# Making the low parts of the down products' weights with an adding transfer in a two-block transformer kernel

## The chip, the core and the metric

The kernel runs on one core of one Trainium2 chip. The metric is the device time of one execution in microseconds (us). Three timed runs of the kernel before gave a median of 1833.34 us (1831.85 to 1833.65).

The engines named below are TensorE (PE in the profile; its weight loads are PEld), VectorE (DVE), ScalarE (ACT), GpSimd (POOL) and SyncE (SP, which here only issues transfers).

## The reference

One sequence of 512 tokens with 1024 features passes through two blocks of two layers each, in float32. The first block has a stick-breaking attention layer and a latent attention layer. In the second block each layer has a mixer (first a sparse one, then a differential one) and then this MLP, which is the part that the change touches:

```python
def sq_relu_mlp(h, w_up, w_down):
    u = jnp.einsum('btd,df->btf', h, w_up)
    return jnp.einsum('btf,fd->btd', jnp.square(jax.nn.relu(u)), w_down)

h = h + sq_relu_mlp(rms_norm_2(h, mlp_norm_g[layer]), mlp_w_up[layer], mlp_w_down[layer])
```

`w_up` is 1024 x 4096 and `w_down` is 4096 x 1024, so each layer has 32 blocks of 128 x 1024 numbers of down weights; there are two layers.

## The kernel before

**Three products for one.** TensorE multiplies in a reduced format (`fp32r`, called FR in the code). To keep float32 accuracy, each matrix is split into a high part (the value rounded to fp32r) and a low part (the value minus its high part), and each product is made of three: high x high, low x high and high x low (the helper `three`). The activations' parts of the MLP are HIDH and HIDL.

**The stream of weight blocks.** Weights come as blocks of 128 x 1024 float32 numbers (512 KB) in one fixed stream, numbered b. For each block

- SP loads the raw numbers into one of two buffers (`load`, WRAW, NR = 2),
- ACT makes the high part in one of three buffers (`split_high`, WH, NS = 3) once TensorE has used block b - 3,
- DVE, or POOL for some blocks outside the MLPs, makes the low part (`split_low`, WL, also three buffers),
- TensorE waits for both parts and uses the block.

A raw buffer may be loaded again when the low part of the block in it is made (`at("low", b - NR)` in `load`).

**The MLP.** A layer's hidden features come in four quarters c = 0 to 3. Quarter 0 goes the plain way: eight up blocks m = 0 to 7 with 24 matmuls of 512 columns each. Its results are scaled by DVE (line 2476), squared and split by ACT (lines 2520 and 2522), and their low parts are made by POOL (line 2552, HIDL<-TMP,HIDH). For m > 3 POOL then also mixes four planes of the input (`plane_mix`, lines 2341, 2344 and 2347), which quarters 1 to 3 need: their up products are made by a fast scheme with fewer matmuls, in eight steps of 42 matmuls of 256 columns (`fast_pe`). Each quarter ends with eight down blocks m = 0 to 7 of 24 matmuls of 512 columns, called down m below. TensorE's order for them is: down 0 without its last two k, down 1 without its last two k, the rest of down 0, the rest of down 1, then down 2 to 7 whole. `low` of the first three down blocks of quarter 0 is made in the last three rounds of `mlp_vector`'s first loop, those of the other quarters in rounds 6 to 8 of its fast loop; the others follow as TensorE frees their buffers.

**Order.** Each engine runs its own list of instructions in the order in which it is written, and waits only at semaphores. The order is written out by hand in `mlp_tensor`, `mlp_vector`, `mlp_scalar` and `mlp_gpsimd`; nothing is planned by costs. POOL has no work in an MLP other than its first loop.

Of the kernel before, what the change touches and what calls it, by code (L numbers as in the profile page):

```python
# [8 lines left out]
F32 = mybir.dt.float32  # L9
FR = mybir.dt.float32r  # L10
BF16 = mybir.dt.bfloat16
ALU = mybir.AluOpType
# [12 lines left out]
NR, NS = 2, 3  # L25
# [111 lines left out]
def program(nc, A, out):  # L137
    ctx = ExitStack()
    with ctx:
# [114 lines left out]
        on_pool |= {block[("o_v", b), half] for b in range(1, 4) for half in range(2)}  # L254

        def load(e, w, b):
            if b >= NR:
                w.wait_ge(*at("low", b - NR))
            name, i, width, _ = stream[b]
            e.dma_start(WRAW[b % NR][:, 0:width], A[name][i]).then_inc(*dma(f"s_w{b % NR}"))  # L260

        def split_high(e, w, b):
            if b >= len(stream):
                return
            n = stream[b][2]
            w.wait_ge(*dma(f"s_w{b % NR}", b // NR + 1))
            if b >= NS:
                w.wait_ge(*at("used", b - NS))
            e.activation(WH[b % NS][:, 0:n], WRAW[b % NR][:, 0:n], ACT.Copy).then_inc(*inc("s_high", ("high", b)))  # L269

        def split_low(e, w, b, pool):
            if b >= len(stream) or (b in on_pool) != pool:
                return
            n = stream[b][2]
            if b >= NS:
                w.wait_ge(*at("used", b - NS))
            w.wait_ge(*at("high", b))
            e.tensor_tensor(WL[b % NS][:, 0:n], WRAW[b % NR][:, 0:n], WH[b % NS][:, 0:n].bitcast(F32),  # L278
                            ALU.subtract).then_inc(*inc("s_low_pool" if pool else "s_low", ("low", b)))
# [26 lines left out]
        def tile_t(e, w, name, m, hi, lo, need, kt=KT):  # L306

            per = BW // (128 * kt)
            b = block[name, m // per]
            wh, wl = (x[b % NS][:, 0:BW].rearrange("p (k n) -> p k n", k=kt) for x in (WH, WL))  # L310
            bank, was = banks.take((name, m), ("evac", name, m))
            w.wait_ge(*at("high", b))
            w.wait_ge(*at("low", b))
            for key in was:
                w.wait_ge(*at(*key))
            c = slice(128 * (m % per), 128 * (m % per) + 128)
            made = three(e, w, bank, [(wh[:, k, c], wl[:, k, c], hi(k), lo(k), need(k)) for k in range(kt)])
            ends = [("used", b)] * (m % per == per - 1)
            made.then_inc(*inc("s_tile", ("tile", name, m), *ends))

        def tile_n(e, w, name, hi, lo, need, cols=256):
# [7 lines left out]
            for half in range(2):  # L329
                b = block[name, half]  # L330
                wh, wl = (x[b % NS][:, 0:BW].rearrange("p (k n) -> p k n", k=4) for x in (WH, WL))
                w.wait_ge(*at("high", b))
                w.wait_ge(*at("low", b))
                for i in range(NT):
                    made = three(e, w, bk[i][:, 0:cols],
                                 [(hi(k)[:, tok[i]], lo(k)[:, tok[i]], wh[:, k % 4, :], wl[:, k % 4, :], need(k))
                                  for k in range(4 * half, 4 * half + 4)], half == 0, half == 1)
                    ends = [("tile", name, i)] * (half == 1) + [("used", b)] * (i == NT - 1)
                    if ends:
                        made.then_inc(*inc("s_tile", *ends))  # L340
# [211 lines left out]
        def out_sets(e, w, name, layer, m, ks, bank=None):  # L552
# [3 lines left out]
            w.wait_ge(*at("high", b))  # L556
            w.wait_ge(*at("low", b))
            if ks[0] == 0:
# [48 lines left out]
        def l0_tensor(e, w):  # L607
# [12 lines left out]
            def linear(name, m):  # L620
# [4 lines left out]
                w.wait_ge(*at("high", b))  # L625
                w.wait_ge(*at("low", b))
                for key in was:
# [394 lines left out]
        def l1_tensor(e, w):  # L1022
# [91 lines left out]
            w.wait_ge(*at("high", b))  # L1114
            w.wait_ge(*at("low", b))
            for i in range(NT):
# [414 lines left out]
        def l2_tensor(e, w):  # L1531
            need = need_h("mix0")

            def linear(t, bank):
# [4 lines left out]
                w.wait_ge(*at("high", b))  # L1539
                w.wait_ge(*at("low", b))  # L1540
                for key in was:
# [12 lines left out]
            def natural(half):  # L1554
# [8 lines left out]
                w.wait_ge(*at("high", b))  # L1563
                w.wait_ge(*at("low", b))
                for i in range(NT):
# [14 lines left out]
            def compress(which, q):  # L1580
# [6 lines left out]
                w.wait_ge(*at("high", b))  # L1587
                w.wait_ge(*at("low", b))
                w.wait_ge(*at("window hi", which))
# [16 lines left out]
            def second(which):  # L1606
# [5 lines left out]
                w.wait_ge(*at("high", b))  # L1612
                w.wait_ge(*at("low", b))
                made = three(e, w, bank[:, 0:62], [(wh[:, k, :], wl[:, k, :], EHH[:, k, :], EHL[:, k, :],
# [818 lines left out]
        def mlp_tensor(e, w, L):  # L2433
# [6 lines left out]
            def down(c, m, ks):  # L2440
                b = block[("dn", L, c), m]
                wh, wl = (x[b % NS][:, 0:BW].rearrange("p (k n) -> p k n", k=KT) for x in (WH, WL))
                w.wait_ge(*at("high", b))
                w.wait_ge(*at("low", b))
                if ks[0] == 0:
# [103 lines left out]
        def mlp_gpsimd(e, w, L):  # L2549
            for m in range(8):  # L2550
# [3 lines left out]
                if m > 3:  # L2554
                    plane_mix(e, w, L, m - 4)


# [61 lines left out]
        def l3_tensor(e, w):  # L2619
# [17 lines left out]
            def linear():  # L2637

                for name, m in o_slots:
                    b = block[name, m]  # L2640
                    w.wait_ge(*at("high", b))
                    w.wait_ge(*at("low", b))
                    if name in ("o_q", "o_k"):
# [474 lines left out]
        def end_tensor(e, w):  # L3118
# [4 lines left out]
            def part(x, ks):  # L3123
# [4 lines left out]
                w.wait_ge(*at("high", b))  # L3128
                w.wait_ge(*at("low", b))
                for k in ks:  # L3130
# [367 lines left out]
```

## Time and profile before

| what | value |
|---|---|
| median of three runs | 1833.34 us |
| the profiled execution | 1832.36 us |
| its span (first to last instruction) | 1830.3 us |
| TensorE busy | 1786.5 us (98%) |
| VectorE busy | 1153.7 us (63%) |
| ScalarE busy | 866.5 us (47%) |
| GpSimd busy | 447.4 us (24%) |
| high parts of weights on ScalarE (line 269) | 214 of 1044 ns |
| low parts of weights on VectorE (line 278) | 201 of 1286 ns |

Matmuls are pipelined, so a busy TensorE is not one at its peak: the distance from one matmul's start to the next's is what a matmul costs. What a wait costs is read from TensorE's rows, since TensorE is the engine that hardly rests. A row of a timeline has the start and the length in us, the engine, the line of the kernel, the operation, what it writes and reads, its shape and count, and in brackets the idle time ahead of it and what ended that. "DMA to landing" is from the issue of a transfer to the moment when its semaphore is full.

### The profile page before, as it was taken

Reading aid. Unit: us, or ns where it says so; the run is one execution under the profiler, and the core shown is the slowest. Engines: PE = TensorE matmul, PEld = TensorE weight load, DVE = VectorE, ACT = ScalarE, POOL = GpSimd, SP = SyncE. Lnnn points to the kernel's source line nnn. Section 1 sums busy time; section 2 is a strip of 40 time slices with the busy share of each in tenths; the row PEclk is TensorE's granted clock in tenths of the full one; section 3 lists DMA queues with packets and bytes.
Section 4 is the critical chain, followed back from the end, with each engine's and each line's share of the span. In section 5 each row is a group of like instructions: output and inputs, shape, how many; then the busy total and the mean of one; then the engine's idle time right before and its main releaser. Section 6 shows DMA issues by size and latency. Waiting matters only on the chain.

```text
span 1830.3 us, 26599 instructions
## 1 busy us (share of the span) xinstructions
PE 1786.5 (98%) x10528; PEld 1466.9 (80%) x10532; DVE 1153.7 (63%) x1869; ACT 866.5 (47%) x1409; POOL 447.4 (24%) x451
## 2 busy tenths in 40 slices
PE   7999999999999999999999999999999999999997
PEld 6987777766678757677889898988888788989896
DVE  5355555575545688854577585765677656858574
ACT  5236665355435465564345352533444534435253
POOL 0035551011311235551140000005678214000000
PEclk9999999999999999999999999999999999999999
DMA  5221111231012421111232322222222123232322
GB/s 183 95 67 50 55 50 58 81 97 53 24 47 89 136 67 36 35 36 58 81 115 93 115 93 104 84 99 83 87 89 76 50 81 127 82 115 93 106 91 81
DMA packets 44522, 149.22 MB, mean 82 GB/s; under 512 B 6000, under 2 KB 6384, under 8 KB 44400
## 3 DMA queue, kind: packets, MB, share of 16 engines
q1 hardware_dynamic: 44400, 147.53, 24.0%
q8 instruction: 84, 1.38, 0.3%
q14 instruction: 38, 0.31, 0.0%
HBM read 139.64 MB, written 2.10 MB: 77 GB/s over the span
## 4 chain that ended last, share of the span: by engine, by line
PE 86%; DVE 6%; ACT 3%; POOL 2%; issue 2%; DMA 0%; POOLq 0%; SPq 0%; DVEq 0%; ACTq 0%
PE BANK L301 18%; PE BANK L303 18%; PE BANK L302 18%; PE BANK L2382 4%; PE BANK L2383 4%; PE BANK L2380 4%; PE BANK L933 3%; PE BANK L667 2%; PE BANK L1717 1%; PE BANK L1698 1%; PE BANK L1674 1%; PE BANK L990 1%; PE BANK L2713 1%; PE BANK L652 1%; PE BANK L2688 1%
## 5 line engine op out<-in xcount | busy, mean ns | idle before, releaser
L269 ACT ACTIVATE WH<-WRAW 128x1024 fp32r<-128x1024 f32 (+1 forms) x214 | 222.9, 1044 | 341.4 <-PE BANK L303 312.5
L278 DVE TENSOR_TENSOR WL<-WRAW,WH 128x1024 fp32r<-128x1024 f32 (+1 forms) x201 | 258.3, 1286 | 131.2 <-ACT WH L269 130.9
L301 PE MATMUL BANK<-HH,WH 128*128 128x512 f32 x664 | 273.1, 411 | 12.0 <-DVE WL L278 9.8
L303 PE MATMUL BANK<-HL,WH 128*128 128x512 f32 x664 | 260.2, 392 | 0.0
L302 PE MATMUL BANK<-HH,WL 128*128 128x512 f32 x664 | 259.9, 391 | 0.0
L301 PE MATMUL BANK<-HIDH,WH 128*128 128x512 f32 (+1 forms) x520 | 201.4, 387 | 1.6 <-issue 1.5
L302 PE MATMUL BANK<-HIDH,WL 128*128 128x512 f32 (+1 forms) x520 | 200.9, 386 | 0.0
L303 PE MATMUL BANK<-HIDL,WH 128*128 128x512 f32 (+1 forms) x520 | 200.8, 386 | 0.0
L2383 PE MATMUL BANK<-HP,G 128*128 128x256 f32 x672 | 190.5, 283 | 0.0
L2382 PE MATMUL BANK<-HP,G 128*128 128x256 f32 x672 | 190.5, 283 | 0.0
L2380 PE MATMUL BANK<-HP,G 128*128 128x256 f32 x672 | 190.4, 283 | 0.0
L495 DVE TENSOR_TENSOR X<-X,BANK 128x512 f32<-128x512 f32 x95 | 65.2, 686 | 167.7 <-PE BANK L303 167.7
L301 PEld LDWEIGHTS BANK<-HH,WH 128*128 128x128 f32 x664 | 125.4, 189 | 46.2 <-issue 21.5
L303 PEld LDWEIGHTS BANK<-HL,WH 128*128 128x128 f32 x664 | 125.1, 188 | 27.0
L302 PEld LDWEIGHTS BANK<-HH,WL 128*128 128x128 f32 x664 | 125.5, 189 | 25.4 <-issue 2.9
L2380 PEld LDWEIGHTS BANK<-HP,G 128*128 128x128 f32 x672 | 129.2, 192 | 0.2
L2382 PEld LDWEIGHTS BANK<-HP,G 128*128 128x128 f32 x672 | 129.2, 192 | 0.2
L2383 PEld LDWEIGHTS BANK<-HP,G 128*128 128x128 f32 x672 | 129.2, 192 | 0.0
L301 PEld LDWEIGHTS BANK<-HIDH,WH 128*128 128x128 f32 x520 | 97.8, 188 | 22.6 <-issue 3.2
L303 PEld LDWEIGHTS BANK<-HIDL,WH 128*128 128x128 f32 x520 | 97.8, 188 | 19.8
L302 PEld LDWEIGHTS BANK<-HIDH,WL 128*128 128x128 f32 x520 | 97.8, 188 | 19.2
L2322 ACT ACTIVATE G<-RAW 128x1792 fp32r<-128x1792 f32 x32 | 54.5, 1703 | 88.2 <-DVE RAW L2314 69.0
(446 smaller groups left out, 3755.3 us busy)
## 6 DMA issues: line engine op xcount, KB each, us to landing
WRAW<-in_w SPq DMA_DIRECT2D x77, 512.0 KB, 3.5
WRAW<-in_wd SPq DMA_DIRECT2D x64, 512.0 KB, 3.5
RAW<-in_wf SPq DMA_DIRECT2D x32, 512.0 KB, 3.6
WRAW<-in_wu SPq DMA_DIRECT2D x16, 512.0 KB, 3.4
TMP<-in_wf SPq DMA_DIRECT2D x16, 512.0 KB, 3.5
WRAW<-in_w0o SPq DMA_DIRECT2D x8, 512.0 KB, 3.5
WRAW<-in_w1o SPq DMA_DIRECT2D x8, 512.0 KB, 3.4
WRAW<-in_wc SPq DMA_DIRECT2D x8, 512.0 KB, 3.4
```

The lines of the kernel that those rows point to most:

```text
L269: e.activation(WH[b % NS][:, 0:n], WRAW[b % NR][:, 0:n], ACT.Copy).then_inc(*inc("s_high", ("high", b)))
L278: e.tensor_tensor(WL[b % NS][:, 0:n], WRAW[b % NR][:, 0:n], WH[b % NS][:, 0:n].bitcast(F32), ALU.subtract).then_inc(*inc("s_low_pool" if p ...
L301: e.matmul(dst, ah, bh, start=first and i == 0, stop=False)
L302: e.matmul(dst, al, bh, start=False, stop=False)
L303: made = e.matmul(dst, ah, bl, start=False, stop=last and i == len(sets) - 1)
L495: e.tensor_tensor(X[:, m, :], X[:, m, :], banks[name, m], ALU.add).then_inc(*inc("s_evac", ("evac", name, m)))
L667: made = e.matmul(l0_bank(h, bk)[:, c0 + 128 * (jj - j):c0 + size[j]], ntri if jj == j else nones, nlf[:, h % 2, col[jj]:col[jj] + size[jj ...
L933: made = e.matmul(bank[:, c], a, b, start=(i == 0), stop=(i == len(sets) - 1), skip_group_check=True)
L2322: e.activation(flat(G[s % 3][:, 0:7, :]), raw_part(s, 1, 7), ACT.Copy).then_inc(*inc("s_fast_high", ("fast high", L, s)))
L2380: e.matmul(dst, wh[:, a, cols], hi, start=half == 0 and j not in started, stop=False, skip_group_check=True)
L2382: e.matmul(dst, wl[:, a, cols], hi, start=False, stop=False, skip_group_check=True)
L2383: made = e.matmul(dst, wh[:, a, cols], lo, start=False, stop=half == 1 and i == 1, skip_group_check=True)
```

## The change

For the 64 down blocks, DVE no longer makes the low part. ACT, right after it has written the high part, writes its negative into the low buffer (a second activation with scale -1, `s_minus`). Then POOL issues a transfer (`add_raw`) that reads the raw block from memory a second time and adds it onto the low buffer, so that this holds raw minus high. TensorE waits for the semaphore of that transfer in place of `low` (`low_made`). SP may reload a raw buffer as soon as the high part of its block is made (`raw_read`). No other block is changed.

```diff
+        added = [b for b, (_, _, _, key) in enumerate(stream) if key[0][0] == "dn"]
+        def low_made(b):
+            if b in added:
+                return dma(f"s_low_added{b % NS}", 1 + sum(a % NS == b % NS for a in added if a < b))
+            return at("low", b)
+        def raw_read(b):
+            return at("high", b) if b in added else at("low", b)
         def load(e, w, b):
             if b >= NR:
-                w.wait_ge(*at("low", b - NR))
+                w.wait_ge(*raw_read(b - NR))
...
         def split_high(e, w, b):
             e.activation(WH[b % NS][:, 0:n], WRAW[b % NR][:, 0:n], ACT.Copy).then_inc(*inc("s_high", ("high", b)))
+            if b in added:
+                w.wait_ge(*at("high", b))
+                e.activation(WL[b % NS][:, 0:n], WH[b % NS][:, 0:n].bitcast(F32), ACT.Copy, scale=-1.0).then_inc(
+                    *inc("s_minus", ("minus high", b)))
+        def add_raw(e, w, b):
+            name, i, n, _ = stream[b]
+            w.wait_ge(*at("minus high", b))
+            e.dma_start(WL[b % NS][:, 0:n], A[name][i], accum_op=ALU.add).then_inc(*dma(f"s_low_added{b % NS}"))
         def split_low(e, w, b, pool):
-            if b >= len(stream) or (b in on_pool) != pool:
+            if b >= len(stream) or b in added or (b in on_pool) != pool:
                 return
...
         def mlp_gpsimd(e, w, L):
                 if m > 3:
                     plane_mix(e, w, L, m - 4)
+                if m > 4:
+                    add_raw(e, w, block[("dn", L, 0), m - 5])
+            for c in range(4):
+                for m in range(8):
+                    if c or m > 2:
+                        add_raw(e, w, block[("dn", L, c), m])
```

Every wait of TensorE for `at("low", b)` became one for `low_made(b)`.

POOL, the end of a layer's first loop (rounds m = 4 to 7), before:

```order
181 L2552 TENSOR_TENSOR HIDL<-TMP,HIDH 128x512 x5
182 L2341 TENSOR_TENSOR STAGE<-STAGE 128x512
183 L2344 TENSOR_TENSOR STAGE<-STAGE 128x256
184 L2347 TENSOR_TENSOR STAGE<-STAGE 128x256
185 L2552 TENSOR_TENSOR HIDL<-TMP,HIDH 128x512
186 L2341 TENSOR_TENSOR STAGE<-STAGE 128x512
187 L2344 TENSOR_TENSOR STAGE<-STAGE 128x256
188 L2347 TENSOR_TENSOR STAGE<-STAGE 128x256
189 L2552 TENSOR_TENSOR HIDL<-TMP,HIDH 128x512
190 L2341 TENSOR_TENSOR STAGE<-STAGE 128x512
191 L2344 TENSOR_TENSOR STAGE<-STAGE 128x256
192 L2347 TENSOR_TENSOR STAGE<-STAGE 128x256
```

The same place on POOL with the change:

```order
185 L2572 TENSOR_TENSOR HIDL<-TMP,HIDH 128x512
186 L2361 TENSOR_TENSOR STAGE<-STAGE 128x512
187 L2364 TENSOR_TENSOR STAGE<-STAGE 128x256
188 L2367 TENSOR_TENSOR STAGE<-STAGE 128x256
189 L289 DMA WL<-in_wd 128x1024
190 L2572 TENSOR_TENSOR HIDL<-TMP,HIDH 128x512
191 L2361 TENSOR_TENSOR STAGE<-STAGE 128x512
192 L2364 TENSOR_TENSOR STAGE<-STAGE 128x256
193 L2367 TENSOR_TENSOR STAGE<-STAGE 128x256
194 L289 DMA WL<-in_wd 128x1024
195 L2572 TENSOR_TENSOR HIDL<-TMP,HIDH 128x512
199 L289 DMA WL<-in_wd 128x1024 x30
```

The first adding transfer stands behind the second plane mix, the second behind the third, and the other thirty of the layer behind the fourth.

ACT, from the last fast steps to the first down blocks of a later quarter, with the change:

```order
594 L2441 ACTIVATE Q<-Q 128x1024
595 L2443 ACTIVATE Q<-Q 128x1024
596 L2445 ACTIVATE HIDH<-Q 128x1024
597 L280 ACTIVATE WH<-WRAW 128x1024
598 L283 ACTIVATE WL<-WH 128x1024
599 L2413 ACTIVATE Q<-BANK 128x256
600 L280 ACTIVATE WH<-WRAW 128x1024
601 L283 ACTIVATE WL<-WH 128x1024
602 L2441 ACTIVATE Q<-Q 128x1024
603 L2443 ACTIVATE Q<-Q 128x1024
604 L2445 ACTIVATE HIDH<-Q 128x1024
605 L280 ACTIVATE WH<-WRAW 128x1024
```

Each high part (line 280, before line 269) is followed at once by its negative (line 283), which is new; the rest keeps its order.

## Rows read from the trace of the kernel before

**Rows 1.** The page: span and busy time of the engines (us, share, count).

```profile
span 1830.3 us, 26599 instructions
PE 1786.5 (98%) x10528; PEld 1466.9 (80%) x10532; DVE 1153.7 (63%) x1869; ACT 866.5 (47%) x1409; POOL 447.4 (24%) x451
```

**Rows 2.** Busy time by stretch: columns PE, PEld, DVE, ACT, POOL, clock, DMA share, GB/s.

```profile
880.00:923.30 43.30, 43.24 (x189) 35.15 (x188) 25.81 (x31) 16.34 (x23) 13.33 (x10) 1.00 0.21 73
923.30:968.20 44.90, 44.14 (x194) 36.28 (x195) 32.57 (x35) 20.83 (x18) 13.40 (x11) 1.00 0.35 128
1008.40:1052.00 43.60, 43.60 (x195) 36.12 (x194) 22.68 (x31) 13.16 (x11) 0.00 (x0) 1.00 0.33 119
```

**Rows 3.** TensorE's timeline where down 0 and down 1 of quarter 0 begin.

```profile
921.04 0.39 PE L301 MATMUL BANK<-HH,WH 128*128 128x512 f32 x1
...
922.85 0.39 PE L303 MATMUL BANK<-HL,WH 128*128 128x512 f32 x1
923.31 0.47 PE L301 MATMUL BANK<-HIDH,WH 128*128 128x512 f32 x1
...
928.43 0.47 PE L301 MATMUL BANK<-HIDH,WH 128*128 128x512 f32 x1 [0.75 <-issue]
```

**Rows 4.** POOL's timeline at the same place (rounds 5 and 6).

```profile
922.08 2.27 POOL L2341 TENSOR_TENSOR STAGE<-STAGE 128x512 f32<-128x512 f32 x1
...
925.25 0.74 POOL L2347 TENSOR_TENSOR STAGE<-STAGE 128x256 f32<-128x256 f32 x1
925.95 1.30 POOL L2552 TENSOR_TENSOR HIDL<-TMP,HIDH 128x512 fp32r<-128x512 f32 x1
```

**Rows 5.** ACT's timeline there: the high part of down 0's block.

```profile
920.65 1.04 ACT L269 ACTIVATE WH<-WRAW 128x1024 fp32r<-128x1024 f32 x1
```

**Rows 6.** DVE's timeline there: the low part of down 1's block.

```profile
926.12 2.21 DVE L278 TENSOR_TENSOR WL<-WRAW,WH 128x1024 fp32r<-128x1024 f32 x1 [2.31 <-ACT WH L269]
```

**Rows 7.** Transfers in 968 to 1052 us: packets, MB, share; KB each, us to landing.

```profile
q1 hardware_dynamic: 2326, 8.45, 28.9%
WRAW<-in_wd SPq DMA_DIRECT2D x8, 512.0 KB, 3.5
```

**Rows 8.** TensorE's timeline where down 0 of quarter 1 begins.

```profile
1008.31 0.40 PE L301 MATMUL BANK<-HIDH,WH 128*128 128x512 f32 x1
```

**Rows 9.** ACT's timeline in quarter 1, from the last fast step on.

```profile
1004.88 1.04 ACT L269 ACTIVATE WH<-WRAW 128x1024 fp32r<-128x1024 f32 x1
...
1009.84 1.06 ACT L2421 ACTIVATE Q<-Q 128x1024 f32<-128x1024 f32 x1 [2.46 <-DVE Q L2415]
1010.94 1.06 ACT L2423 ACTIVATE Q<-Q 128x1024 f32<-128x1024 f32 x1
...
1018.11 1.06 ACT L269 ACTIVATE WH<-WRAW 128x1024 fp32r<-128x1024 f32 x1 [5.02 <-PE BANK L303]
```

**Rows 10.** TensorE's first matmuls, after 9.78 us of idle time.

```profile
9.78 0.76 PE L301 MATMUL BANK<-HH,WH 128*128 128x512 f32 x1 [9.78 <-DVE WL L278]
10.35 0.63 PE L302 MATMUL BANK<-HH,WL 128*128 128x512 f32 x1
...
13.70 0.40 PE L301 MATMUL BANK<-HH,WH 128*128 128x512 f32 x1
```

**Rows 11.** Busy time by stretch after TensorE's last matmul (columns as rows 2).

```profile
1822.00:1822.50 0.50, 0.00 (x0) 0.00 (x0) 0.29 (x2) 0.47 (x2) 0.00 (x0) 1.00 0.00 0
1823.00:1823.50 0.50, 0.00 (x0) 0.00 (x0) 0.50 (x3) 0.00 (x0) 0.50 (x2) 0.50 0.00 0
```

**Rows 12.** POOL's timeline in the second layer: the end of its second plane mix.

```profile
1524.04 0.74 POOL L2347 TENSOR_TENSOR STAGE<-STAGE 128x256 f32<-128x256 f32 x1
```

**Rows 13.** TensorE's timeline in the second layer: the start of its down 0.

```profile
1522.09 0.47 PE L301 MATMUL BANK<-HIDH,WH 128*128 128x512 f32 x1
```

**Rows 14.** The issue of a plain transfer on SP.

```profile
1043.83 0.33 SPq L2304 DMA_DIRECT2D TMP<-in_wf  x1
```

**Rows 15.** Transfers of the whole execution: the four that load X at its start.

```profile
X<-in_x SPq DMA_DIRECT2D x4, 512.0 KB, 6.9
```

More of the change, by code:

```diff
@@ L312, in tile_t @@
             w.wait_ge(*at("high", b))
-            w.wait_ge(*at("low", b))
+            w.wait_ge(*low_made(b))
             for key in was:
@@ L332, in tile_n @@
                 w.wait_ge(*at("high", b))
-                w.wait_ge(*at("low", b))
+                w.wait_ge(*low_made(b))
                 for i in range(NT):
@@ L556, in out_sets @@
             w.wait_ge(*at("high", b))
-            w.wait_ge(*at("low", b))
+            w.wait_ge(*low_made(b))
             if ks[0] == 0:
@@ L625, in linear @@
                 w.wait_ge(*at("high", b))
-                w.wait_ge(*at("low", b))
+                w.wait_ge(*low_made(b))
                 for key in was:
@@ L1114, in l1_tensor @@
             w.wait_ge(*at("high", b))
-            w.wait_ge(*at("low", b))
+            w.wait_ge(*low_made(b))
             for i in range(NT):
@@ L1539, in linear @@
                 w.wait_ge(*at("high", b))
-                w.wait_ge(*at("low", b))
+                w.wait_ge(*low_made(b))
                 for key in was:
@@ L1563, in natural @@
                 w.wait_ge(*at("high", b))
-                w.wait_ge(*at("low", b))
+                w.wait_ge(*low_made(b))
                 for i in range(NT):
@@ L1587, in compress @@
                 w.wait_ge(*at("high", b))
-                w.wait_ge(*at("low", b))
+                w.wait_ge(*low_made(b))
                 w.wait_ge(*at("window hi", which))
@@ L1612, in second @@
                 w.wait_ge(*at("high", b))
-                w.wait_ge(*at("low", b))
+                w.wait_ge(*low_made(b))
                 made = three(e, w, bank[:, 0:62], [(wh[:, k, :], wl[:, k, :], EHH[:, k, :], EHL[:, k, :],
@@ L2443, in down @@
                 w.wait_ge(*at("high", b))
-                w.wait_ge(*at("low", b))
+                w.wait_ge(*low_made(b))
                 if ks[0] == 0:
@@ L2641, in linear @@
                     w.wait_ge(*at("high", b))
-                    w.wait_ge(*at("low", b))
+                    w.wait_ge(*low_made(b))
                     if name in ("o_q", "o_k"):
@@ L3128, in part @@
                 w.wait_ge(*at("high", b))
-                w.wait_ge(*at("low", b))
+                w.wait_ge(*low_made(b))
                 for k in ks:
```

## The prediction, made before the changed kernel was run

> **What bounds the kernel.** I read the page first. TensorE is busy for 1786.5 of 1830.3 us; DVE, which loses work, for 63% [rows 1]. So time taken off DVE is worth only what TensorE waits for DVE. I then cut the MLP of layer 0 into stretches [rows 2]: up tiles (880 to 923.3), down tiles of quarter 0 (923.3 to 968.2), down tiles of quarter 1 (1008.4 to 1052). TensorE has work in all of 43.3, in 44.14 of 44.9 and in all of 43.6 us. A matmul of 512 columns costs (922.85 - 921.04) / 8 = 0.226 us [rows 3], 24 of them 5.44 us, and eight tiles 43.5. Quarter 1 takes just that, quarter 0 some 1.3 more. TensorE's timeline shows where: about 0.2 us ahead of down 0 at 923.31, and 0.75 ahead of down 1 at 928.43 [rows 3]. The latter is the wait for its low part, which DVE ends at 926.12 + 2.21 = 928.33 [rows 6]. That is all DVE can give back: about 1 us a layer, 2 in all. What counts is whether the new chain for the low part is as early as the old.
>
> **What goes and comes.** DVE loses 64 instructions of some 1.2 to 2.2 us, which the above says is worth at most 2 us, and only if nothing later takes the wait's place. ACT gains 64 of 1.06 us. In the 43.6 us of quarter 1's down tiles ACT is busy for 13.16 [rows 2]; the new ones add 8.5 at most, so its throughput is no issue, only its place in the chain. SP's loads may start a DVE instruction earlier; nothing waits for them. POOL issues 64 transfers. DMA is 33% busy in that stretch [rows 2]: 2326 packets of queue 1 are 8.45 MB, 16 transfers of 512 KB, in 0.289 x 84 us, so one keeps the 16 engines busy for 1.5 us [rows 7]. An adding one reads memory and the buffer: 3.0. With the load, 4.5 per 5.44 us: it fits, with little to spare.
>
> **The unknown, D.** D is the time from POOL's reaching an adding transfer to its full semaphore. The trace has none, nor any transfer issued by POOL. Nearest: a plain one of the same size takes 3.5 us [rows 7]. That is the lower end, as adding needs all that a copy needs and a second read. The four loads of X at the start, which share the engines with others, take 6.9 [rows 15]; that is not an upper bound, since how fast the adder is, and how POOL makes its orders, no row shows. As an outer end I take 8.3, at which (below) the chain would fill the time between three blocks; beyond it the loss grows faster. Between the ends I add: 3.5, plus 1.5 for the second read, plus about 1.0 for sharing with the plain load that the new rule releases at nearly the same moment. D = 6.0. POOL itself is held for q per issue: SP's issue takes 0.33 [rows 14], I take 1.0, at most 2.0.
>
> What memory moves is a matter for a page: in the Trainium skill, "Collectives: The Full Stack" (the bandwidth ceiling) says that the add costs no cycles but two reads on one ring, which halves the rate; "DMA: Bandwidth & Descriptors" (Latency) gives a transfer issued by GpSimd about 2 us plus its bytes over 436 GB/s. An estimate from both pages is 2 + 2 x 1.2 = 4.4 us, and the sum below would end at 1849. No run here shows it yet.
>
> **Quarter 0, twice.** This is where order counts. POOL's new list has the first transfer behind its second plane mix. That mix ends at 925.95, 2.64 us after TensorE stood ready for down 0 at 923.31 [rows 3, 4]. The negative is no obstacle: the high part starts at 920.65 and takes 1.04 [rows 5], two of them end at about 922.9. In before DVE had made this low part by then. So down 0 starts at 925.95 + D = 931.95. POOL goes on with a HIDL of 1.29 and a mix of 925.95 - 922.08 = 3.8 [rows 4], so the second transfer comes q + 5.12 later, at 932.07, and lands at 938.07; the third comes at 938.2.
>
> TensorE has rested for 8.6 us. At the kernel's start, after 9.78 us without work, its first nine matmuls are 0.43 us apart (1.2 GHz) before the distance becomes 0.23 (2.4 GHz): 3.92 us for what takes 2.04 [rows 10]; after its last matmul the granted clock is 1.00 at 1822.0 and 0.50 at 1823.0 [rows 11]. So I charge 1.9 us for slow matmuls. By the Trainium skill, "TensorE: Matmul & The Clock Gate" (Part 1), an idle array falls to half its clock; those rows agree. Without that rule the sum would be at most 3.8 less.
>
> Down 0 without its last two k is 18 matmuls: 4.08 + 1.9, to 937.93. Down 1 waits to 938.07, runs to 942.15. The rests end at 943.5 and 944.9; down 2 runs 944.9 to 950.3. The buffer of down 3 is free at 943.5; as in quarter 1 the high part starts 0.28 later, two activations take 1.10 + 1.06 [rows 9], POOL gets the signal 0.06 later, and it lands at 952.0. Down 3 started at 968.2 - 0.3 - 5 x 5.44 = 940.7 in before; now at 952.0: 11.3 us late. Downs 4 to 7 have 10.88 us from free buffer to use, less 0.28 + 2.16 + 0.06, so they hold up to D = 8.3 and wait for nothing. The second layer repeats it: the mix ends at 1524.78, TensorE is ready at 1522.09 [rows 12, 13]. Twice 11.3 = 22.6.
>
> **Quarters 1 to 3, six times.** Down 0 starts at 1008.31 [rows 8]. Two places are tight. Down 1, due 4.08 us later at 1012.39: its high part starts at 1004.88 [rows 9], its negative is ready at 1007.1, so 5.3 us are there for D. Down 3, due at 1008.31 + 72 x 0.2267 = 1024.63: since TensorE interleaves downs 0 and 1, its buffer is free only at 1017.8; the high part starts at 1018.11, the negative is ready at 1020.3, 4.3 us are there. In before, DVE needed 1.2. At D = 6: 0.7 + 1.7 = 2.4 us, six times: 14.4. These waits are short; I charge no clock.
>
> **The sum.** 22.6 + 14.4 = 37.0. The profiled execution took 1832.36, so 1869.4; the median shown is 1.0 above it: 1870. The same steps for other D: 3.5 gives 14.2 (1847), 5.0 gives 22.8 (1855), 7.0 gives 53.1 (1885), 8.3 gives 73.9 (1906), 10 gives 114 (1946). If q is 2.0, add 2 us.
>
> **Rivals.**
> First, a quick transfer (D under 5): only quarter 0's place behind the mixes costs. For it: the plain one's 3.5, and engines 67% idle. 1847 to 1855. 20%.
> Second, the middle, D from 5 to 7.5: 1855 to 1893, my forecast. 52%.
> Third, the transfer becomes a bound (D over 7.5, or over 5.4 us of the engines' time): then most downs wait, not two per quarter, and each us of D over 8.3 costs about 24 us, (114 - 73.9) / 1.7. For it: nothing in the trace shows the adder's rate. Against: the engines have two thirds of their time. 1893 to 1950 or more. 24%.
> Fourth, not slower: POOL reaches the transfer in time. It would have to land by 923.3, so with the lowest D the second mix would have to end at 919.8, 6.2 us before the 925.95 of the rows and 2.3 us before that mix begins at 922.08 [rows 4]. Then quarter 0 gives its 1 us back, and if D is below 4.3 the rest costs nothing: 1833.3 - 2 = 1831. It decides at the order of POOL's list alone, and that order is against it. 3%.
> That the change doesn't do what it says (a block still split by DVE) is excluded by the lists; the last 1% is for what I have not thought of.
>
> **Chances and range.** What a measurement of this kernel can tell from no change is about 0.2%, 3.7 us. The first three all lie over it: 96% slower, 2% the same, 2% faster. The range reaches from the first's lower edge to 1925, some way into the third; 15% are left out, nearly all above.
>
> **What would show it.** In the profile after: TensorE's first matmul of down 0 in quarter 0 waits 6 to 9 us for the transfer of WL, in both layers, and the next nine or so are 0.43 apart; POOL's issue stands directly behind the second mix. In later quarters down 1 and down 3 wait, the others not. The line of adding transfers gives D's landing time: near 6 if I am right. TensorE's wait for DVE at down 1 is gone. I am wrong if down 0 doesn't wait (order), if waits stand at every down tile (D or the rate too low), or if the plain loads' 3.5 us grow beyond 5, which would move waits to the high parts.

## The result and the profile after

The changed kernel takes 1908.47 us, the median of four runs (1905.14 to 1911.56); the kernel before took 1832.74 us in four runs beside it. The ratio is 1.040, with a 95% interval of 1.038 to 1.042. It is slower by 76 us where 37 were forecast. The profiled execution took 1905.14 us.

The page of the changed kernel: span, busy time of the engines, the queues, TensorE's largest group, the adding transfers (line 289; what ended POOL's idle time before them), and two lines of its list of transfers (count, KB each, median us from issue to landing).

```profile
span 1903.3 us, 26667 instructions
PE 1803.9 (95%) x10532; PEld 1474.6 (77%) x10532; DVE 1074.5 (56%) x1805; ACT 932.2 (49%) x1473; POOL 498.1 (26%) x515
...
q1 hardware_dynamic: 44400, 147.53, 23.8%
q0 software_dynamic: 9216, 33.56, 10.0%
...
L321 PE MATMUL BANK<-HIDH,WH 128*128 128x512 f32 (+1 forms) x520 | 208.5, 401 | 57.7 <-issue 53.7
...
L289 POOL DMA_DIRECT2D WL<-in_wd x64 | 55.9, 874 | 564.9 <-ACT WL L283 564.9
...
WRAW<-in_wd SPq DMA_DIRECT2D x64, 512.0 KB, 4.3
...
WL<-in_wd POOLq DMA_DIRECT2D x64, 512.0 KB, 7.4
```

Against [rows 1], DVE gave 79 us of busy time and ACT took 66, as meant, and neither shows in the time. The span grew by 73.0 us, TensorE's busy time by 17.4. A matmul's busy time is counted longer while the clock is low, so this is a first sign of slow matmuls; the remaining 55.6 us are rest. Queue 0 is the adding transfers: 33.56 MB in 64 pieces, 0.100 x 1903.3 / 64 = 2.97 us of all 16 engines for each. From issue to landing one takes 7.4 us in the median (5.1 to 10.3). The plain loads of the same blocks now take 4.3 instead of 3.5 [rows 7].

The view of waits names 14 large waits in a group that it could put down to nothing (issue), 53.7 us together, the longest 10.3:

```profile
PE BANK L321 <- issue: 53.7, 14, 10.3
```

TensorE's timeline shows what they are. Columns: start, length, engine, line, operation, and in brackets the rest before it and what ended it.

```profile
922.69 0.39 PE L323 MATMUL BANK<-HL,WH 128*128 128x512 f32 x1
933.43 0.77 PE L321 MATMUL BANK<-HIDH,WH 128*128 128x512 f32 x1 [10.35 <-issue]
933.99 0.63 PE L322 MATMUL BANK<-HIDH,WL 128*128 128x512 f32 x1
934.42 0.63 PE L323 MATMUL BANK<-HIDL,WH 128*128 128x512 f32 x1
...
953.66 0.47 PE L321 MATMUL BANK<-HIDH,WH 128*128 128x512 f32 x1 [1.59 <-issue]
965.60 0.47 PE L321 MATMUL BANK<-HIDH,WH 128*128 128x512 f32 x1 [0.73 <-DMA WL<-in_wd]
1029.11 0.47 PE L321 MATMUL BANK<-HIDH,WH 128*128 128x512 f32 x1 [2.49 <-issue]
1046.90 0.69 PE L321 MATMUL BANK<-HIDH,WH 128*128 128x512 f32 x1 [3.67 <-issue]
1139.03 0.66 PE L321 MATMUL BANK<-HIDH,WH 128*128 128x512 f32 x1 [3.84 <-issue]
1567.71 0.77 PE L321 MATMUL BANK<-HIDH,WH 128*128 128x512 f32 x1 [9.12 <-issue]
```

The first row is the last up tile of quarter 0, the second is down 0, 10.5 us late. 953.66 is down 3 and 965.60 down 5 of quarter 0. 1029.11 is down 1 and 1046.90 down 3 of quarter 1; 1139.03 is down 3 of quarter 2. The last row is down 0 of quarter 0 in the second layer. POOL's timeline holds the other side:

```profile
920.67 1.30 POOL L2572 TENSOR_TENSOR HIDL<-TMP,HIDH 128x512 fp32r<-128x512 f32 x1 [1.41 <-ACT HIDH L2542]
921.93 1.29 POOL L2361 TENSOR_TENSOR STAGE<-STAGE 128x512 f32<-128x512 f32 x1
923.30 0.73 POOL L2364 TENSOR_TENSOR STAGE<-STAGE 128x256 f32<-128x256 f32 x1
924.11 0.72 POOL L2367 TENSOR_TENSOR STAGE<-STAGE 128x256 f32<-128x256 f32 x1
924.78 1.02 POOL L289 DMA_DIRECT2D WL<-in_wd  x1
929.88 0.87 POOL L289 DMA_DIRECT2D WL<-in_wd  x1
...
1021.54 0.86 POOL L289 DMA_DIRECT2D WL<-in_wd  x1 [6.63 <-ACT WL L283]
...
1039.03 0.88 POOL L289 DMA_DIRECT2D WL<-in_wd  x1 [14.31 <-ACT WL L283]
```

The first transfer stands directly behind the second mix, as the order of the list has it. It is issued at 924.78 and lands 8.6 us later, when down 0 starts. The one issued at 1021.54 lands 7.5 us later, at 1029.0, and down 1 starts at 1029.11. The one at 1039.03 takes 7.8, to 1046.8, and down 3 starts at 1046.90. Whatever the view calls them, the 17 waits of 0.7 us and more in the two MLPs all end 0.09 to 0.13 us after an adding transfer has landed.

The granted clock, in three stretches (columns as in [rows 2]):

```profile
925.00:926.00 1.00, 0.00 (x0) 0.00 (x0) 0.00 (x0) 1.00 (x2) 1.00 (x2) 1.00 0.38 61
927.00:928.00 1.00, 0.00 (x0) 0.00 (x0) 0.00 (x0) 0.98 (x2) 1.00 (x2) 0.76 0.97 242
1029.00:1031.00 2.00, 1.89 (x6) 1.60 (x7) 0.00 (x0) 0.00 (x0) 0.00 (x0) 0.73 0.92 182
```

TensorE rested from 923.1 and the clock fell from its upper level (2.4 GHz) to the lower (1.2 GHz) within 927 to 928. After the 2.5 us of rest ahead of 1029.11 it fell as well, on the way through 1029 to 1031. From 1029.88 to 1033.26 the matmuls start 0.43 us apart, in place of 0.23.

Adding up the starts of TensorE's matmuls over both MLPs gives the balance. The waits, counted from start to start less the usual distance of 0.23, are 60.4 us (24.3 in the two quarters 0, 36.0 in the six later ones), the slow matmuls cost 14.0 (4.4 and 9.6), and before had 2.2 of both. 60.4 + 14.0 - 2.2 = 72.2, of the 73.0 by which the span grew. Slow matmuls follow both long waits and six of the twelve waits at down 1 and down 3 of the later quarters.

### The profile page after: what moved, and what is told of

It reads as the page before. It is cut to its first block, busy times and chain, and to the rows that moved or that the text cites. A ratio compares the mean times of both kernels' runs of the same rounds, so it can differ in the third digit from the quotient of the medians.

```text
span 1903.3 us, 26667 instructions
## 1 busy us (share of the span) xinstructions
PE 1803.9 (95%) x10532; PEld 1474.6 (77%) x10532; DVE 1074.5 (56%) x1805; ACT 932.2 (49%) x1473; POOL 498.1 (26%) x515
## 3 DMA queue, kind: packets, MB, share of 16 engines
q0 software_dynamic: 9216, 33.56, 10.0%
## 4 chain that ended last, share of the span: by engine, by line
PE 78%; DVE 7%; ACT 6%; issue 5%; POOL 2%; DMA 2%; POOLq 0%; SPq 0%; DVEq 0%; ACTq 0%
PE BANK L321 16%; PE BANK L322 15%; PE BANK L323 15%; PE BANK L2403 4%; PE BANK L2402 4%; PE BANK L2400 4%; PE BANK L953 2%; PE BANK L687 2%; ACT WH L280 2%; DVE WL L298 1%; PE BANK L1737 1%; PE BANK L1718 1%; PE BANK L1694 1%; PE BANK L1010 1%; PE BANK L2739 1%
## 5 line engine op out<-in xcount | busy, mean ns | idle before, releaser
L321 PE MATMUL BANK<-HIDH,WH 128*128 128x512 f32 (+1 forms) x520 | 208.5, 401 | 57.7 <-issue 53.7
L298 DVE TENSOR_TENSOR WL<-WRAW,WH 128x1024 fp32r<-128x1024 f32 (+2 forms) x137 | 173.7, 1269 | 104.9 <-ACT WH L280 104.1
L322 PE MATMUL BANK<-HIDH,WL 128*128 128x512 f32 (+1 forms) x520 | 206.3, 397 | 0.0
L323 PE MATMUL BANK<-HIDL,WH 128*128 128x512 f32 (+1 forms) x520 | 205.4, 395 | 0.0
L289 POOL DMA_DIRECT2D WL<-in_wd x64 | 55.9, 874 | 564.9 <-ACT WL L283 564.9
```

What stands on the lines that cost most here:

```text
L289: e.dma_start(WL[b % NS][:, 0:n], A[name][i], accum_op=ALU.add).then_inc(*dma(f"s_low_added{b % NS}"))
L321: e.matmul(dst, ah, bh, start=first and i == 0, stop=False)
L322: e.matmul(dst, al, bh, start=False, stop=False)
L323: made = e.matmul(dst, ah, bl, start=False, stop=last and i == len(sets) - 1)
```

## The experiments

The kernel before took 1832.6 to 1833.4 us on the chips used. Where no interval stands, a kernel ran once; after's four runs lie within 3.4 us of their median, so I read nothing from less than about 5 us; experiment 3 shows how much of that is the clock.

**1. The first transfer ahead of the mix**

```diff
-                if m > 3:
-                    plane_mix(e, w, L, m - 4)
                 if m > 4:
                     add_raw(e, w, block[("dn", L, 0), m - 5])
+                if m > 3:
+                    plane_mix(e, w, L, m - 4)
```

> The changed kernel with POOL's first three adding transfers ahead of the plane mix of their round, not behind it. If the place in POOL's list decides when down 0 of quarter 0 starts: the first transfer is issued when its negative is ready, at about 922.7 instead of 924.8, and down 0 starts about 2.1 us earlier in each layer; about 4 us less in all, 1901 against 1905. If ACT's chain (or the transfer's own length) decided alone and POOL's order did not matter: the first issue stays within 0.5 us of 924.8 and the time within 1 us of 1905.

1902.48 us, 6 under after's median and 2.7 under its profiled execution. POOL's first issue, and TensorE's start of down 0:

```profile
922.88 1.03 POOL L289 DMA_DIRECT2D WL<-in_wd  x1 [0.99 <-ACT WL L283]
```
```profile
929.02 0.77 PE L321 MATMUL BANK<-HIDH,WH 128*128 128x512 f32 x1 [6.03 <-issue]
```

The issue now waits for the negative (922.88) and no longer for the mix (924.78). Down 0 starts 4.4 us sooner: 1.9 of them are the order, 2.5 are this transfer's length, 6.1 instead of 8.6. That length differs from run to run: it is 7.1, 7.7 and 7.9 in experiments 3, 6 and 7, whose edits don't touch POOL's list or the plain loads. Waits and slow matmuls of the two quarters 0 are 6 us less together. In the six later quarters, which have the same instructions as after, they are 3 us more, nearly all of it slow matmuls, and this is within what differs from run to run. The order costs a few us; it isn't where the 76 went.

**2. A plain copy in place of the addition** (the low part is then the raw weight)

```diff
-            e.dma_start(WL[b % NS][:, 0:n], A[name][i], accum_op=ALU.add)
+            e.dma_start(WL[b % NS][:, 0:n], A[name][i])
```

> The changed kernel with POOL's transfers as plain copies of the raw weights into the low buffer, in the same place, with the same waits, without the adding (the low parts are then not the low parts). If the second read that adding needs, and the engines' time for it, makes the transfer long: one alone lands after about 3.7 to 4.2 us instead of 5.2, the ones in bursts after about 5 instead of 7.5, each takes half the engines' time (1.5 us instead of 3.0), and the kernel takes about 1855 (the sum of the prediction at 5). If POOL's way of issuing is what is long: landing stays at 5 alone and 7 in bursts, and the kernel takes 1895 or more.

1874.58 us: between the two expectations. The page and the view of this line:

```profile
q0 software_dynamic: 9216, 33.56, 5.9%
...
L289 POOL DMA_DIRECT2D WL<-in_wd x64 | 34.5, 539 | 550.7 <-ACT WL L283 550.7
...
DMA to landing us min/median/max: 3.6/4.8/9.0
```

A copy issued by POOL takes 3.7 us alone, almost what SP's take [rows 7], and 0.059 x 1872.6 / 64 = 1.7 us of the engines against 2.97 with the addition. At down 1 and down 3 of quarter 1 it takes 5.8 and 5.6 us, against 7.5 and 7.8. So some 34 of the 76 us are the adding, and some 42 remain with a copy of the same bytes through the same chain.

**3. Source and destination of one type**

```diff
-            e.dma_start(WL[b % NS][:, 0:n], A[name][i], accum_op=ALU.add)
+            e.dma_start(WL[b % NS][:, 0:n], A[name][i].bitcast(FR), accum_op=ALU.add)
```

> The changed kernel with the source of the adding transfer named in the low buffer's own type (fp32r), so that no conversion of type is asked for; the bits added are the same. If the conversion were what makes the transfer long, one alone would land in under 4.5 us and the kernel take 1880 or less. If only reads and writes count: the same landing times within 0.3 us (5.2 alone, 7.4 median) and 1905 within 4.

1909.01 us, and landing in 7.2 us in the median. That the transfer goes from float32 to fp32r costs nothing that these runs can tell.

The run shows one thing more. Its waits are 55.7 us, 4.7 less than in after's profiled execution, but its slow matmuls cost 22 us and not 14.0. So what the clock takes differs by some 8 us between two executions with nearly the same waits. After's own four runs go with it: 1905.14 us at a mean granted clock of 0.988, 1911.56 at 0.984.

**4. One adding transfer at a time**

```diff
             w.wait_ge(*at("minus high", b))
+            if b - 1 in added:
+                w.wait_ge(*low_made(b - 1))
             e.dma_start(WL[b % NS][:, 0:n], A[name][i], accum_op=ALU.add)
```

> The changed kernel, but POOL issues an adding transfer only when the one before it has landed. If bursts on the 16 engines make those of down 1 and down 3 long (7.5 to 7.9 us, while one alone takes 5.2): these two fall to about 6, TensorE waits some 1.5 to 2 us less at each, and with six quarters the kernel takes about 1885. If a transfer's length is its own (issuing, latency), they stay at 7.5 and the kernel takes 1905 or more, since later ones are now issued later.

1943.47 us. That is on the side of the second expectation, but I had expected neither this size nor this place, and its reason, a length of the transfer's own, does not stand either (experiments 9 and 10). POOL's issues for downs 1, 2 and 4 of quarter 1:

```profile
1026.44 0.86 POOL L291 DMA_DIRECT2D WL<-in_wd  x1 [6.62 <-ACT WL L283]
1034.64 0.86 POOL L291 DMA_DIRECT2D WL<-in_wd  x1 [7.33 <-DMA WL<-in_wd]
...
1052.20 0.88 POOL L291 DMA_DIRECT2D WL<-in_wd  x1 [7.25 <-DMA WL<-in_wd]
```

Down 1's still takes 7.6 us, though no other adding transfer is in flight; down 2's, held back until that has landed, takes 5.3. So another adding transfer is not the neighbour that makes down 1's long. Holding each one back makes the later ones late: down 4's could have gone out at 1050.5 and went out at 1052.20, beside three loads of the fast steps' weights; it took 9.3 us. New waits came up at down 4, of 1.4 to 3.2 us in five of the later quarters and of 4.8 and 4.9 in the quarters 0.

**5. DVE makes the tight ones again**: down 1 and down 3 everywhere, and down 0 of quarter 0; 46 blocks are left to the transfer

```diff
-        added = [b for b, (_, _, _, key) in enumerate(stream) if key[0][0] == "dn"]
+        added = [b for b, (_, _, _, key) in enumerate(stream) if key[0][0] == "dn"
+                 and key[1] not in (1, 3) and not (key[0][2] == 0 and key[1] == 0)]
...
         def add_raw(e, w, b):
+            if b not in added:
+                return
```

> The changed kernel, but DVE makes the low parts of down 1 and down 3 in every quarter and of down 0 in quarter 0, as before the change; the other 46 of 64 blocks still go by transfer. If the loss sits in the few places where the chain is longer than TensorE's cover: nearly all of it goes, 1833 within 4. If the transfers' amount (the engines' rate, POOL, ACT's extra instruction) costs: two thirds of the loss stay in proportion to the blocks, 1880 or more.

1863.55 us, a ratio of 1.0175 (1.016 to 1.019). It gives back 45 of the 76 us, not all. In quarter 0, POOL and TensorE show what is late next:

```profile
935.50 1.04 POOL L292 DMA_DIRECT2D WL<-in_wd  x1
```
```profile
941.36 0.76 PE L324 MATMUL BANK<-HIDH,WH 128*128 128x512 f32 x1 [5.56 <-issue]
```

The first transfer is now down 2's. It stands behind POOL's fourth mix in the list, goes out at 935.50, takes 5.8 and down 2 waits for it. Down 5 waits too, 1.2 to 2.5 us, in the quarters 0 to 2 of both layers: in quarter 1 its transfer goes out at 1037.12 beside three loads of the fast steps' weights and takes 10.4 us. I had priced these places by their room in after, in which TensorE itself ran late.

**6. Work in the waits**: 36 matmuls whose result is thrown away ahead of down 0 of quarter 0, and 8 ahead of down 1 and down 3 of the others

```diff
-                w.wait_ge(*low_made(b))
                 if ks[0] == 0:
...
+                    more = {0: 36 if c == 0 else 0, 1: 8 if c else 0, 3: 8 if c else 0}.get(m, 0)
+                    if more:
+                        w.wait_ge(*at("hid hi", L, c, 0))
+                    for _ in range(more):
+                        e.matmul(banks[("dn", L, c), m], wh[:, 0, :], hid_plane(0, 0), start=True, stop=True,
+                                 skip_group_check=True)
+                w.wait_ge(*low_made(b))
```

> The changed kernel with extra matmuls whose results are thrown away, put ahead of TensorE's wait for the low part: 36 at down 0 of quarter 0 and 8 at down 1 and at down 3 of the other quarters (about 8.2 and 1.8 us at full clock, less than the waits of 10 and 2.5 to 3.8 us there). If half of the time lost beside the waits is the slow clock after them: the matmuls behind the waits are 0.23 us apart, not 0.43, and of the 14 us of slow matmuls 10 or more go: 1895 or less. If the slow matmuls are not caused by the rest ahead of them: 1905, or more by what the extra matmuls cost.

1891.42 us: 17 us less than after's median and 13.7 less than its profiled execution, though TensorE does more. TensorE at down 1 of quarter 1:

```profile
1024.73 1.97 PE L2472 MATMUL BANK<-HIDH,WH 128*128 128x512 f32 x8
1027.70 0.50 PE L321 MATMUL BANK<-HIDH,WH 128*128 128x512 f32 x1 [0.99 <-DMA WL<-in_wd]
1028.03 0.39 PE L322 MATMUL BANK<-HIDH,WL 128*128 128x512 f32 x1
1028.26 0.40 PE L323 MATMUL BANK<-HIDL,WH 128*128 128x512 f32 x1
```

From the last useful matmul, at 1024.51, to the first of down 1 it is 3.19 us, no less than the 2.88 of after, but the matmuls behind it are 0.23 us apart and not 0.43. Slow matmuls cost 2.8 us in all instead of 14.0 (22 in experiment 3), and these 11 us are most of the 13.7. So the slow matmuls are the clock's answer to the rest ahead of them.

**7. The products with the low part last**: TensorE waits for the low part of a down block only behind its other sixteen matmuls

```diff
-                w.wait_ge(*low_made(b))
...
+                for k in ks:
...
+                    e.matmul(dst, wh[:, k, :], hid_plane(k, 0), start=k == 0, stop=False)
+                    e.matmul(dst, wh[:, k, :], hid_plane(k, 1), start=False, stop=False)
+                w.wait_ge(*low_made(b))
+                for k in ks:
+                    made = e.matmul(dst, wl[:, k, :], hid_plane(k, 0), start=False, stop=k == 7)
```

> The changed kernel, but each down tile does its two products with the high part of the weights for all its k first and the ones with the low part last, and waits for the low part only before these. That gives the transfer 16 of 24 matmuls more, 3.6 us (2.7 where only six k are done). If what counts is when TensorE asks for the low part: the waits at down 1 and down 3 (2.6 and 3.8 us) all but go in the six later quarters, down 0 of quarter 0 still waits about 7.8 us in each layer and some slow matmuls stay there: about 1852. If instead the transfers' rate were the limit, the waits would only move: 1890 or more.

1851.78 us, a ratio of 1.0112 (1.0097 to 1.0127), as expected. Of the waits in layer 0's MLP this is left (from 920 to 1300 us):

```profile
PE BANK L2476 <- DMA WL<-in_wd: 7.2, 2, 7.0
```

The new order gives each chain 3.6 us more (16 matmuls; 2.7 us at down 0 and down 1, which begin with six of their eight k), and the waits of the layer's later quarters are gone but for 0.2 us. Quarter 0's 7.0 us stay (6.4 in the second layer), and with some 5 us of slow matmuls they are most of the 19 us that this kernel still loses.

**8. The same order in the kernel before**, with DVE's low parts

> The kernel before the change with the same order of products in its down tiles (the ones with the low part last). Its only waits in the MLPs are 0.9 us at down 1 of quarter 0 in each layer. If these go, 1.8 us less, 1830.6 in the profiled run, 0.1%; and nothing more. If the order of the matmuls had a price of its own (switching between buffers), it would be slower by more than 4.

1832.94 us, a ratio of 1.0003 (0.9992 to 1.0014). The wait for DVE's low part [rows 3] is gone, and in its place, in each layer, stands

```profile
PE BANK L2452 <- POOL HIDL L2556: 0.7, 1, 0.7
```

DVE's part of the chain was worth nothing by itself: POOL's low part of the activations was due at the same time.

**9. Small plain loads**: SP loads 64 of 1024 columns of each down block (their high part is then mostly left from another block; the addition stays whole)

```diff
+            if b in added:
+                e.dma_start(WRAW[b % NR][:, 0:64], A[name][i][:, 0:64]).then_inc(*dma(f"s_w{b % NR}"))
+                return
             e.dma_start(WRAW[b % NR][:, 0:width], A[name][i]).then_inc(*dma(f"s_w{b % NR}"))
```

> The changed kernel, but SP's plain loads of the down blocks bring only 64 of 1024 columns (ACT makes the high parts of what then lies in the buffer; the products are not the reference's). Every instruction and wait stays. If an adding transfer is slow at down 1 and down 3 because it shares the 16 engines with a plain load that is released at the same moment: with the loads all but gone those land after 5.3 to 5.9 us as the lone ones do, TensorE's waits there fall from 2.6 and 3.8 us to under 1 and 1.6, and the kernel takes 1855 to 1865. If its length is its own or POOL's: the landing stays at 7.5 and the kernel at 1895 or more.

1872.39 us. The landing time is as expected:

```profile
DMA to landing us min/median/max: 5.3/5.6/10.3
```

At down 1 of quarter 1 it is 5.4 us, at down 3 5.8, against 7.5 and 7.8 in after. The median's 7.4 is thus an adding transfer beside a plain load, and 5.1 to 5.6 is one by itself. The small load pays too: at down 1 it is issued 0.89 us behind the addition and lands 4.7 us later, 0.2 us after it. The kernel gains less than I expected: down 0 of quarter 0 still waits 7.4 and 7.1 us, down 3 of the later quarters still waits 1.5 to 2.4 where I had expected under 1.6, and slow matmuls still cost 6.9.

**10. Small adding transfers**: 64 of 1024 columns are added (the rest of the low buffer stays the negated high part)

```diff
-            e.dma_start(WL[b % NS][:, 0:n], A[name][i], accum_op=ALU.add)
+            e.dma_start(WL[b % NS][:, 0:64], A[name][i][:, 0:64], accum_op=ALU.add)
```

> The changed kernel, but each adding transfer adds only 64 of 1024 columns (the rest of the low buffer stays the negated high part; the products are not the reference's). What is left of the landing time is the part that does not grow with bytes. If most of the lone one's 5.2 us is bytes read twice (3.0 us of engine time): 2.5 to 3.2 us, and only down 0 of quarter 0 still waits; the kernel takes 1842 to 1848. If most of it is POOL's issuing (0.9 us) and latency: 4 us or more.

1848.97 us. The list of transfers and the view of the line:

```profile
WL<-in_wd POOLq DMA_DIRECT2D x64, 32.0 KB, 2.6
...
DMA to landing us min/median/max: 2.4/2.6/6.8
```

2.4 us is what an addition takes that moves next to nothing. But at down 1 and down 3, where a plain load runs at the same time, even this small one takes 4.5 and 5.0. So the 7.5 at down 1 has three parts: 2.4 fixed, 2.9 for 512 KB read twice (5.3 - 2.4), and 2.2 from the plain load beside it, whatever the size of the addition.

The packets show part of how. At down 2 of quarter 0, alone, all 144 packets of the small addition start 1.5 to 2.2 us behind its issue (935.66). At down 1 of quarter 1 (issued at 1014.24) 88 of them start in that stretch; 52 more are spread over the next 1.7 us, in which 113 packets of the load start too, and the addition lands 0.17 us ahead of the load. So the two loads of work go side by side, and the small one ends with the large one, as the small load did in experiment 9.

What is left in the time is mostly down 0 of quarter 0, which waits 5.5 us in the first layer and 5.6 in the second; its transfer takes 3.7 and 3.8 us beside two plain loads. With the slow matmuls behind them that makes 15 us. Down 3 of the later quarters still waits four times, 0.5 to 1.0 us each; the view of waits from 920 to 1300 us has two of them:

```profile
PE BANK L321 <- issue: 1.5, 2, 0.8
```

All this the chain and POOL's order cost with an addition of next to no bytes.

**11. More blocks back to DVE**: as 5, with down 2 of quarter 0 and down 5 everywhere; 38 are left

```diff
-                 and key[1] not in (1, 3) and not (key[0][2] == 0 and key[1] == 0)]
+                 and key[1] not in ((1, 3, 5) if key[0][2] else (0, 1, 2, 5))]
```

> The changed kernel, but DVE makes the low parts of down 0, 1, 2 and 5 in quarter 0 and of down 1, 3 and 5 in the others; 38 of 64 blocks go by transfer. If the 30 us that were left when DVE made down 0, 1 and 3 are again single places (down 2, whose transfer stands behind the last plane mix, and down 5, which meets the three loads for the fast steps): under 1837, with no wait over 1 us. If they are the price of the transfers' number: 1855 or more.

1841.11 us, above the 1837 that I had expected at most. Beside the kernel before's own wait at down 1, one is left per layer, at down 3 of quarter 0. TensorE, and POOL ahead of it:

```profile
945.01 0.47 PE L324 MATMUL BANK<-HIDH,WH 128*128 128x512 f32 x1 [2.79 <-issue]
```

```profile
936.80 2.40 POOL L2370 TENSOR_TENSOR STAGE<-STAGE 128x256 f32<-128x256 f32 x1
939.15 1.03 POOL L292 DMA_DIRECT2D WL<-in_wd  x1
```

Its negative was ready at 937.7, but in POOL's list the transfer stands behind the fourth mix, whose last part took 2.40 us here and 0.74 in experiment 5. It went out at 939.15 and took 5.8. So this is POOL's order once more. 38 transfers cost some 8 us where 64 cost 76: the price is set by the places, not by the number.

**12. The order alone, without a transfer**: 8, with POOL's four mixes behind all eight HIDL, and DVE's low part one round later in the up tiles

```diff
-                if m > 3:
-                    plane_mix(e, w, L, m - 4)
+            for p in range(4):
+                plane_mix(e, w, L, p)
...
-                split_low(e, w, after_block(("up", L, 0), m), False)
+                if m:
+                    split_low(e, w, after_block(("up", L, 0), m - 1), False)
...
+            split_low(e, w, after_block(("up", L, 0), 7), False)
```

> The kernel before the change with the product with the low part last, with POOL's four plane mixes behind all eight HIDL of the layer, and with DVE's low part of a block one round later in the up tiles, so that the scaling of an up tile no longer stands behind a low part that waits for ACT. If the 1.3 us that TensorE rests at the start of the down tiles of quarter 0 in each layer hang on these chains alone: 2 to 2.6 us less, 1828 in the profiled run, a ratio of 0.9985 to 0.999. If the next chain (the mixed planes, the high parts) takes over: within 1 us of before.

1829.26 us, the median of ten runs, against 1833.06 of before: a ratio of 0.998 (0.997 to 0.9989). TensorE in quarter 0, columns as in [rows 2]:

```profile
923.00:968.00 45.00, 45.00 (x208) 37.61 (x207) 33.77 (x35) 18.99 (x15) 19.34 (x13) 1.00 0.34 117
```

It is busy in all of it, where before had 44.14 of 44.9 [rows 2]. Of all kernels here this one has the lowest time, but only just: 3.8 us under before, by the interval 2 to 5.5 us. It needs neither the second read nor the negatives. Which of its changes of order brings the gain was not taken apart; experiment 8 shows that the order of the products alone brings nothing.

## Why the prediction came out as it did

The sign, the mechanism and both kinds of places were right, and the time lies inside the range. But 76 us is twice the forecast's 37, and is out of the forecast's own case (1855 to 1893); it lies in the times of the third. That the range holds it is owed to its width, up to 1925, and not to the sum, which gave 1870.

- **What bounds the kernel: right.** 79 us off DVE brought nothing. The at most 2 us that I allowed were too many: experiment 8 took the wait for DVE away and POOL's HIDL stood at the same place.
- **Quarter 0: right in place, 22.6 forecast, 26.5 measured** (24.3 of waits, 4.4 of slow matmuls, less before's 2.2). Down 0 was to start at 931.95 and started at 933.43. Two errors partly cancel, by luck. The mix ended 1.2 us sooner than [rows 4] had it: its first part takes 1.29 us and not 2.27, now that DVE makes no low part beside it. In experiment 5, where DVE does, it takes 2.27 again. And D was 8.6, not 6.0. By the Trainium skill, "SBUF — State Buffer" (Who interferes with whom), an instruction of VectorE with two inputs in the buffer contends with one of GpSimd that reads it; these rows agree.
- **Quarters 1 to 3: right in place, 14.4 forecast, about 46 measured. This step failed by its sizes.** Down 1 and down 3 wait in each of the six quarters, and the others hold, as the room of 5.3 and 4.3 us said. With D = 7.5 and 7.8 they give 2.2 + 3.5 = 5.7 us a quarter, 34 in six; 36.0 were measured.
- **D: forecast 6.0 = 3.5 + 1.5 + 1.0; measured 7.4 in the median.** The parts for a lone transfer were near: 5.0 against 5.1 to 5.6. The 1.0 for the plain load beside it is the part that failed: it is 2.2 (experiments 9 and 10). No row stood behind the 1.0. Experiment 10 shows that a neighbour of 1.5 us of engine time holds up even an addition of 32 KB by 1.6 to 2.6. A room of 5.3 and 4.3 us makes a small error in D a large one in the time: D - room goes from 0.7 and 1.7 to 2.2 and 3.5. The prediction's own list shows it: 37 us at 6.0, 53 at 7.0, 74 at 8.3.
- **"These waits are short; I charge no clock": wrong.** The clock fell in or just behind six of the twelve short waits too, all six between 2.5 and 3.8 us long: the slow matmuls in the six quarters cost 9.6 us in this execution. Experiment 6 shows it, since work in the waits takes the slow matmuls away. For quarter 0 I had charged 3.8 in both layers and 4.4 were measured.
- **q, the issue on POOL: right**, 1.02 us for the first and 0.87 for the others, against 1.0. **Engine time: right**, 2.97 against 3.0. By the Trainium skill, "Collectives: The Full Stack" (the bandwidth ceiling), the add itself costs no cycles and its price is the second read; 1.7 us for the copy against 2.97 point the same way. The estimate of 4.4 us from it and from the Trainium skill, "DMA: Bandwidth & Descriptors" (Anatomy of one DMA, where the formula stands), does not hold here: 5.1 is the least of 64, 7.4 their median.
- **The third rival had the time and not the mechanism.** It wanted D over 7.5 and waits at most downs. D was about 7.5 and the waits stayed at two tiles a quarter, and one more in quarter 0: down 5, whose transfer took 10.3 us beside three loads of fast-step weights. The forecast had downs 4 to 7 holding up to 8.3, which is consistent with that; where downs 4 and 5 took 8.5 to 9.0 in later quarters they held all the same: TensorE, held up at down 3, came late to them itself.
- **The fourth rival (not slower)** fell at POOL's order, as said; and experiment 10 shows that even an addition of 32 KB, which took 3.7 us there, loses 13 us at that place (15.1 less before's 2.2).

What stays open is why a plain load costs its neighbour more than its own time on the engines: the packets of the two are seen side by side, but no run here shows what sets their order. Nor was it tried to hold the plain load back until the addition has landed.

## What to carry to other kernels

Work taken off an engine that nobody waits for is worth nothing, while the chain that takes its place is paid for wherever it has less room than it needs: work out, tile by tile, the time from the free buffer to the first use, and set the new latency against the least of them. Price a transfer in the company that it will have, not alone: here it took 5.3 us alone, 7.5 beside one load and 10.4 beside three. Where the room is tight, first ask whether the consumer can use the late operand last; that gave 57 of the 76 us back for a change of order.

## What the runs showed of the hardware

- An adding transfer issued by GpSimd, 512 KB of float32: 5.1 to 5.6 us to landing alone, 2.97 us of the 16 engines, 0.87 us of GpSimd for the issue. A plain one issued by GpSimd: 3.7, 1.7 and 0.54 us. One of 32 KB that adds: 2.4 us.
- With a plain load of 512 KB issued 0.6 to 1.1 us behind it the adding one takes 7.2 to 7.9 us (eleven cases in after's profile), and the one of 32 KB 4.0 to 5.0. Where that load came 1.6 us behind (down 3 of quarter 3), the large one took 5.5 and the small one 2.6. Beside three loads of other weights the large one takes 8.5 to 10.6 and the small one 6.2 to 6.8.
- Adding from float32 into fp32r took no longer than within one type, as far as these runs can tell (7.4 and 7.2 us).
- TensorE's granted clock fell in, or up to 0.8 us behind, six of twelve waits of 1.6 to 3.8 us, and the matmuls were then 0.43 us apart (1.2 GHz), behind 1029.11 until 1033.26. Waits of nearly one length differ in this: behind 2.49 us at 1029.11 it fell, behind 2.65 us in the second layer it did not, as the rows of after show:

```profile
1662.91 0.47 PE L321 MATMUL BANK<-HIDH,WH 128*128 128x512 f32 x1 [2.65 <-issue]
1663.21 0.40 PE L322 MATMUL BANK<-HIDH,WL 128*128 128x512 f32 x1
1663.45 0.39 PE L323 MATMUL BANK<-HIDL,WH 128*128 128x512 f32 x1
```

- A two-input instruction of GpSimd on 128 x 512 float32 (the mix's TENSOR_TENSOR) took 2.27 to 2.33 us wherever VectorE was making a low part when it began (all eight in before, six in experiment 5), and 1.29 to 1.30 where VectorE was not or began later (experiments 5 and 12). In after the two mixes of each layer that follow an adding transfer took 1.52 to 1.59.
